# Two attention stages of a two-block kernel: the filler products start right behind the first scores

## The reference

```
def first_block(...):
    y_ssd = ssd_mixer(z, xbc, dt_raw, ...)
    y_att = chunk_attention(q, k, v, rel_bias[l])        # 8 heads of 64, causal by chunks
    x = x + g_m * (jnp.concatenate([y_ssd, y_att], axis=-1) @ w_out[l])
...
def second_block(...):
    proj = h @ w_in[l]
    qa, ka, va, qm, km, vm, om, gm, mg = split_cols(proj, IN_SPLITS_2)
    ya = windowed_gqa(qa, ka, va, ...)                   # 8 heads, window of 128 to each side
    ym = mlstm_branch(qm, km, vm, om, gm, ...)
```

## Time and profile before

| what | before |
|---|---|
| median of 3 runs | 1814.84 us (1812.18 to 1818.27) |
| the profiled execution | 1817.8 us, span 1815.8 us |
| PE busy | 1730.4 us, 95% of the span |
| DVE busy | 695.8 us, 38% |
| ACT busy | 329.3 us, 18% |
| mean granted clock of PE | 0.977 of full speed |

### The profile page before, as it was taken

How to read it: one execution, slowest core, us unless ns; L and a number is a source line. 1 busy time by engine, 2 the same in 40 slices (tenths; PEclk the granted TensorE clock), 3 DMA queues, 4 the chain that set the end, 5 groups by cost and what they waited for, 6 DMA issues and landing times.

```text
span 1815.8 us, 18461 instructions
## 1 busy us (share of the span) xinstructions
PE 1730.4 (95%) x7272; PEld 954.6 (53%) x7272; DVE 695.8 (38%) x1576; ACT 329.3 (18%) x681; POOL 18.7 (1%) x39
## 2 busy tenths in 40 slices
PE   7999899979999999989999999999889999999997
PEld 3445444468888854435444454444454554545452
DVE  4332347677777721030498232312331211212123
ACT  1121224221111110010133433210300000000000
POOL 0001000000000000000000000000000000000001
PEclk8999999999999999999899999999989999999999
DMA  9676110011222222232111110222389999999997
GB/s 403 250 283 210 52 53 40 33 46 48 92 92 92 70 113 74 85 127 93 53 47 47 47 47 1 93 93 93 139 323 410 427 429 429 429 428 429 429 427 315
DMA packets 30239, 335.50 MB, mean 185 GB/s; under 512 B 3208, under 2 KB 5784, under 8 KB 10592
## 3 DMA queue, kind: packets, MB, share of 16 engines
q1 hardware_dynamic: 22464, 310.56, 42.4%
q10 hardware_dynamic: 5168, 14.91, 2.1%
q0 software_dynamic: 2544, 9.18, 1.4%
HBM read 319.66 MB, written 18.37 MB: 186 GB/s over the span
## 4 chain that ended last, share of the span: by engine, by line
PE 82%; DVE 7%; DMA 6%; ACT 3%; issue 1%; POOL 0%; DVEq 0%; SPq 0%; ACTq 0%; POOLq 0%
PE bank L1315 15%; PE bank L963 14%; PE bank L606 10%; PE bank L999 8%; PE bank L1324 6%; PE bank L1124 5%; PE bank L1132 3%; PE bank L778 3%; PE bank L1082 2%; DMA arena<-in_w_expert_up 2%; DMA slot<-in_w_expert_up 2%; PE bank L922 2%; PE bank L588 2%; PE bank L768 2%; PE bank L940 2%
## 5 line engine op out<-in xcount | busy, mean ns | idle before, releaser
L1315 PE MATMUL bank<-slot,arena 128*64 128x512 f32 x704 | 234.7, 599 | 5.5 <-DMA upper<-in_w_expert_up 3.8
L1315 PE MATMUL bank<-upper,arena 128*64 128x512 f32 x352 | 156.3, 599 | 1.9 <-DMA arena<-in_w_expert_up 1.9
L999 PE MATMUL bank<-arena,slot 128*128 128x512 f32 x352 | 151.2, 592 | 0.0
L606 PE MATMUL bank<-hT,slot 128*128 128x512 f32 x272 | 126.7, 626 | 9.2 <-DVE hT L1845 6.5
L1324 PE MATMUL bank<-arena 128*128 128x128 f32 x1024 | 122.9, 280 | 8.5 <-DVE arena L2098 8.5
L1324 PEld LDWEIGHTS bank<-arena 128*128 128x128 f32 x1024 | 118.6, 195 | 20.8 <-issue 12.2
L1315 PEld LDWEIGHTS bank<-slot,arena 128*64 128x64 f32 x704 | 73.0, 138 | 106.2 <-issue 101.3
L2131 DVE TENSOR_TENSOR arena<-arena,bank 128x512 f32<-128x512 f32 x16 | 11.0, 687 | 283.8 <-PE bank L1315 283.8
L1124 PE MATMUL bank<-hT,slot 128*128 128x512 f32 x256 | 114.5, 595 | 1.9 <-DVE arena L1945 1.9
L999 PEld LDWEIGHTS bank<-arena,slot 128*128 128x128 f32 x352 | 67.0, 190 | 83.6 <-issue 83.6
L606 PEld LDWEIGHTS bank<-hT,slot 128*128 128x128 f32 x272 | 53.9, 201 | 79.9 <-issue 75.0
(11 more groups left out here) (401 smaller groups left out, 2217.2 us busy)
## 6 DMA issues: line engine op xcount, KB each, us to landing
slot<-in_w_expert_gate SPq DMA_DIRECT2D x17, 2048.0 KB, 24.5
slot<-in_w_expert_down SPq DMA_DIRECT2D x16, 2048.0 KB, 27.8
slot<-in_w_in SPq DMA_DIRECT2D x15, 2048.0 KB, 8.0
slot<-in_w_ada SPq DMA_DIRECT2D x12, 2048.0 KB, 13.4
slot<-in_w_up SPq DMA_DIRECT2D x11, 2048.0 KB, 8.1
slot<-in_w_expert_up SPq DMA_DIRECT2D x11, 2048.0 KB, 23.3
upper<-in_w_expert_up SPq DMA_DIRECT2D x11, 2048.0 KB, 26.9
upper<-in_w_expert_down SPq DMA_DIRECT2D x6, 2048.0 KB, 28.6
```

The costliest lines, as they stand in the source:

```text
L606: ins = pe.matmul(bank[home[g]][:, :], w[:, k, c0:c0 + P], src[:, k, :], start=(k == 0), stop=(k == KD - 1))
L999: ins = pe.matmul(bank[j][:, :], w[:, k, :], actT[:, k, :], start=(k == 0), stop=(k == FT - 1))
L1315: ins = pe.matmul(dst[b * CAP:(b + 1) * CAP, :], lhs(b, k), rhs(b, k), start=(k == 0), stop=(k == n_k - 1))
```

## The change

PE's program alone is changed, in the loop that both attentions share. B(0) now comes right behind S(0), before S(1). In each turn of the loop B(2j+1) takes the place of B(2j), and B(2j+2) that of B(2j+1). The last turn has no filler between V(14) and V(15). Every product, wait and semaphore count stays; the programs of DVE, ACT, POOL and SP are the same.

```diff
                 scores(0)
+                between(0)
                 for j in range(NI // 2):
                     if j + 1 < NI // 2:
                         scores(j + 1)
-                    between(2 * j)
+                    between(2 * j + 1)
                     turn(2 * j)
                     turn(2 * j + 1)
                     if j >= 1:
                         values(j - 1)
-                    between(2 * j + 1)
+                    if j + 1 < NI // 2:
+                        between(2 * j + 2)
                 values(NI // 2 - 1)
```

## The result

| what | before | changed |
|---|---|---|
| median of 20 runs each | 1816.4 us (1811.5 to 1818.3) | 1819.1 us (1815.5 to 1824.5) |
| ratio, changed to before | | 1.0026 [1.0018, 1.0035] |
| the profiled execution | 1817.8 us, span 1815.8 | 1817.4 us, span 1815.4 |

The changed kernel is slower: 1816.4 us times the ratio's excess is 4.7 us, with an interval from 3.3 to 6.4. The ratio isn't the quotient of the two medians, which are 2.7 us apart; the means of the 20 runs are 4.6 us apart.

The account below looks back on a forecast made before the run. PE was taken to bound both attentions, with the second's end shifting the program's end one to one through the DMA-bound expert stage. Terms -0.5 + 1.5 + 1.7 = +2.7 us on 1814.84 gave 1817.5 us, range 1812.5 to 1821.0.

Parts of the forecast that it names:

- 3.3, 1.6 and 0.1 us: Second attention: PE's waits for ACT to empty filler banks at B(8), B(16) and B(24), groups 3, 6 and 9.
- the clock falls behind the first wait: Second attention, behind the 3.3 us wait at B(8): granted clock falls, +1.7 us, bounds 0 and 3.5.
- the forecast's 0.5: Second attention: DVE gets the scores of S(5) 0.5 us late, since S(5) stands behind the waiting B(8).
- 1.5 + 1.7: Second attention: ends 1.5 us later at full clock, plus 1.7 us for the clock's fall in the new gap.
- the term of the first attention: First attention's start: gap of 1.08 us becomes 0.31, clock falls as before; -0.5 us, bounds 0 and -0.77.
- rival E: First attention: clock comes back early or never falls, saving 1.7 to 3.5 us; 1812.3 to 1814.1 us, chance 0.10.
- the step to the verdict: Whole kernel: 5.4 us, about 0.3%, taken as what a measurement can tell from no change; forecast no difference.
- The sum: Whole kernel: -0.5 + 1.5 + 1.7 = +2.7 us.
- C: Whole kernel, the forecast: waits and one fall of the clock in the second attention; 1817.5 us, chance 0.40.
- A: Plain gain: banks free in time, only the two attentions' starts change; -4.1 us, 1810.7 us, chance 0.06.
- B: Second attention: the waits without a fall of the clock; +1.0 us in all, 1815.8 us, chance 0.33.
- D: Slower: clock falls behind both waits, B(8) (3.5 us) and B(16) (1.7 us); +6.2 us, 1821.0 us, chance 0.11.

Follow-up runs that it names:

- the products in the hole: Changed kernel plus three extra unread products ahead of B(8)'s wait and one ahead of B(16)'s: ratio 1.0014 to the kernel before, second attention 127.48 us.
- both edits: ACT's emptying ahead of the exponentials plus six extra products in the net's wait: new order 0.9980, old order 0.9993, new order in second attention only 0.9983.
- the net's wait is filled: Six extra products ahead of PE's 2.9 us wait in the feed-forward net: 0.9988 on the kernel before, 1.0014 on the changed kernel.

## Why the prediction was right and wrong

**Right: where and how long PE waits.** Forecast 3.3, 1.6 and 0.1 us at B(8), B(16) and B(24); measured 3.48, 1.75 and 0.21, each within 0.2 us. B(8) was to start 926.55 - 893.09 = 33.46 us behind S(0) and did at 33.50. The reason holds too: the emptying kept its distance from S(0) to 0.01 us, and putting it earlier took the waits away. That a waiting B(8) holds up S(5), which stands behind it and lacks nothing, is seen in DVE's pause of 2.13 us.

**Right: the clock falls behind the first wait and not behind the second.** Forecast 1.7 us, measured 4.42 - 2.84 = 1.58, and 1.6 by the products in the hole. DVE's bias of S(5) is thereby 928.16 - 889.29 = 38.87 us behind S(0), 2.2 later than before: the forecast's 0.5 plus this. At S(9) DVE's pause was 0.48 us, where about 0.5 was forecast.

**Right: the second attention.** Forecast 1.5 + 1.7 = +3.2 us; +3.48 in the profile, +3.6 in the run of it alone.

**Wrong: the term of the first attention.** It was -0.5 us with a clock that falls as before. In the profile the attention is 2.2 us shorter, because the clock was back at 272 us (rival E's mechanism: 1.00 over 272 to 276, where the earlier trace rows has 0.52 over 269 to 276). The size goes with whether the clock is already down at S(0), which the order doesn't decide. Where S(0) took 0.49 us, the attention is 68.42 to 68.45 us long in five profiles with the new order and 70.59 and 70.68 in two with the old: -2.2. Where it took 0.80 us, it is 68.98 to 69.19 in three and 69.57 to 69.70 in four: -0.6, the forecast's size. But neither gain is seen in the time. First and way together are 623.0 us in the mean of the six profiles with the old order there and 623.1 in the eight with the new; single ones lie between 620.9 and 626.2, so this mean alone can't tell 1 us. The ratios say the same: 1.0007 for the new order there alone, and 0.9980 against 0.9983 with and without it once both edits are in. The best value for this term is 0, to within about 2 us. The prediction said of the second attention why a shift passes (the expert stage), and nothing on what lies between the two attentions.

**Wrong: the step to the verdict.** "About 0.3%, 5.4 us, is what a measurement of this kernel can tell from no change, so my forecast is: no difference." Twenty runs of each kernel gave an interval of 3.1 us in width, which excludes 0 at +4.7. A forecast of +2.7 or +3.2 us was worth the word slower at that resolution, and the prediction gave "slower" a chance of only 0.11. Its 5.4 us has no working; it is near the spread of the three single runs (1812.2 to 1818.3), which isn't the resolution of a comparison of many. The sum had the right sign, and this step turned it into "no difference".

**The size.** The time forecast, 1817.5 us, came from the median of 3 runs, 1.6 us under that of the 20. The medians differ by the forecast's 2.7 us, which is luck: each kernel's times lie in more than one heap, and the ratio says 4.7 (3.3 to 6.4). The second attention's 3.5 us lie in that interval; what is above them is open. Take the second attention's length from each profile, and -2.2 us where the net's wait is filled: in the eleven comparisons from which the -2.2 was not taken, this sum lies 0.1 to 1.8 us under the ratio (mean 1.3), 1.2 us for the change and 1.6 us where only the emptying was moved and the order is the old one. So this residue, if it is one, doesn't belong to the new order alone, and no run here tells what it is.

**The rivals.** In the second attention it was C, the forecast. A was refuted by the wait at 922.79, and B, the waits without a fall of the clock, by B(8)'s 4.42 us. D's first fall was to last 7 us and cost 3.5; it cost 1.6. Its second, behind B(16), didn't come: B(17) to T(8) ran at full rate (959.99 to 962.66). E's early return of the clock came in the first attention, without a gain that lasts. So "slower" came true by C's sum and not by D's.

## What to carry to other kernels

Filler that is moved earlier reaches its next full bank earlier as well: follow each move to the point where the buffer is given back, and ask what that engine does first (here exponentials that wait for DVE). Move both ends, the producer and the emptying, or neither: here the one alone lost 3.5 us of the stage, the other alone gave 0.3, and both gave 2.7. And where medians differ by less than the scatter of single runs, predict from the interval that many runs would have, and judge stage lengths rather than spans.

## What the runs showed of the hardware that was not expected

- The same wait of PE (2.90 to 2.92 us, in the net behind the first attention) was followed by sixteen instructions in 3.72 us in six profiles and in 5.41, 6.70 and 6.72 us in three, with PE's work around it unchanged. A window of the run with the second attention alone, at full clock, and one with the first alone, at half:

```profile
412.00:416.00 4.00, 4.00 (x20) 3.52 (x19) 2.79 (x6) 0.00 (x0) 0.00 (x0) 1.00 0.00 0
```

```profile
412.00:416.00 4.00, 4.00 (x11) 3.11 (x11) 2.14 (x4) 0.00 (x0) 0.00 (x0) 0.50 0.00 0
```

- Six products that compute nothing, put ahead of that wait, made the old kernel faster by 2.2 us (0.5 to 3.8). At the places with waits of 0.7 and 1.63 us shown above the clock stayed at 1.00 and the products behind took their full-rate time.
- A shorter first attention went with more half-rate time behind it, in the old order too. The 32 instructions behind PE's idle time of 6.6 us took 8.53 and 8.55 us in the two profiles of the old order with an attention of 70.6 and 70.7 us, and 9.54 to 9.60 us in the four with one of 69.6 to 69.7 us. With the new order they took 9.58 to 9.64 us where S(0) took 0.49 us and 9.75 to 9.83 us where it took 0.80. The rows before and in the changed kernel:

```profile
375.65 8.53 PE L963 MATMUL bank<-hT,slot 128*128 128x256 f32 x32 [6.60 <-ACT hT L2204]
```

```profile
372.73 9.64 PE L965 MATMUL bank<-hT,slot 128*128 128x256 f32 x32 [6.59 <-ACT hT L2206]
```
